# Expert rows gathered in partition quarters and turned on VectorE instead of TensorE, with empty lanes skipped

## What is computed

```
def routed_expert_mlps(x, expert_ids, gates, w_gate, w_up, w_down):
    ...
    def expert_block(args):
        tb, eb = args
        xb = x[tb]
        h = jax.nn.silu(xb @ w_gate[eb]) * (xb @ w_up[eb])
        return h @ w_down[eb]
```

## Time and profile before

| | |
|---|---|
| median of 3 runs | 2599.76 us |
| profiled execution | 2603.91 us, its span 2602.2 us |
| TensorE busy | 2333.2 us (90%) |
| VectorE, ScalarE, GpSimd busy | 1027.2, 707.5, 456.6 us |
| DMA moved | 440.35 MB, mean 169 GB/s |
| granted TensorE clock, mean over the span | 0.952 of full |

### The profile page before, as it was taken

One profiled execution on the slowest core, in us unless ns is written; L12 is line 12 of the kernel. 1 busy time (PEld: TensorE's weight loads), 2 busy tenths in 40 slices (PEclk: granted clock), 3 DMA queues, 4 the chain that ended last, 5 costly groups with the idle time before them and its releaser, 6 DMA issues. The chain is left out here.

```text
span 2602.2 us, 36339 instructions
## 1 busy us (share of the span) xinstructions
PE 2333.2 (90%) x13208; PEld 1339.2 (51%) x13208; DVE 1027.2 (39%) x1762; ACT 707.5 (27%) x1825; POOL 456.6 (18%) x632
## 2 busy tenths in 40 slices
PE   7999999999968999999999999849999999999940
PEld 3454454533546666666667666524444444444420
DVE  4415234224226554456656656341111211112128
ACT  3203122012025544345444554201111111111112
POOL 1010100100200011200131311212222212212235
PEclk9999999999978999899999999969999999999975
DMA  8041230400373112121122111167999999999967
GB/s 283 26 134 33 57 103 9 131 11 11 97 226 76 56 61 88 52 65 56 56 79 88 56 56 61 60 250 297 367 362 361 363 369 370 361 362 361 354 249 314
DMA packets 165971, 440.35 MB, mean 169 GB/s; under 512 B 36961, under 2 KB 78169, under 8 KB 141225
## 3 DMA queue, kind: packets, MB, share of 16 engines
q1 hardware_dynamic: 139351, 350.38, 37.7%
q0 software_dynamic: 20640, 70.29, 6.8%
q10 hardware_dynamic: 5842, 17.80, 1.8%
HBM read 345.11 MB, written 94.80 MB: 169 GB/s over the span
## 5 line engine op out<-in xcount | busy, mean ns | idle before, releaser
L867 PE MATMUL p_ps<-p_xt,p_w 128*128 128x512 f32 x1088 | 476.7, 597 | 0.5 <-DVE p_xt L698 0.5
L3056 PE MATMUL p_ps<-p_w_arena,p_x_arena 128*128 128x512 f32 x1024 | 446.6, 594 | 0.0
L867 PEld LDWEIGHTS p_ps<-p_xt,p_w 128*128 128x128 f32 x1088 | 205.2, 191 | 255.2 <-issue 250.0
L3056 PEld LDWEIGHTS p_ps<-p_w_arena,p_x_arena 128*128 128x128 f32 x1024 | 195.5, 191 | 245.4 <-issue 245.4
L2426 PE MATMUL p_ps<-p_w_out,p_mixt 128*128 128x512 f32 x544 | 252.5, 609 | 0.0
L3072 PE MATMUL p_ps<-p_w_arena,p_y_arena 128*128 128x512 f32 x512 | 236.0, 604 | 0.0
L2978 DVE SCALAR_TENSOR_TENSOR p_y_arena<-p_y_arena,p_ps 128x256 f32<-128x256 f32 x64 | 27.0, 422 | 459.9 <-ACT p_y_arena L2863 358.2
L2426 PEld LDWEIGHTS p_ps<-p_w_out,p_mixt 128*128 128x128 f32 x544 | 99.6, 193 | 105.8 <-issue 103.7
L876 PE MATMUL p_ps<-p_w,p_xt 128*128 128x144 f32 (+1 forms) x512 | 146.6, 440 | 0.0
L2807 POOL DMA_INDIRECT s_y<-p_y_arena,p_home x66 | 65.0, 985 | 462.3 <-PE p_ps L3043 266.6
L3072 PEld LDWEIGHTS p_ps<-p_w_arena,p_y_arena 128*128 128x128 f32 x512 | 93.1, 192 | 98.2 <-issue 93.0
(11 more groups left out here) (415 smaller groups left out, 3254.1 us busy)
## 6 DMA issues: line engine op xcount, KB each, us to landing
p_w_arena<-in_w_exp_gate SPq DMA_DIRECT2D x64, 1024.0 KB, 7.9
p_w_arena<-in_w_exp_up SPq DMA_DIRECT2D x64, 1024.0 KB, 11.1
p_w_arena<-in_w_exp_down SPq DMA_DIRECT2D x64, 1024.0 KB, 10.6
p_w_arena<-s_y SPq DMA_DIRECT2D x16, 1024.0 KB, 13.3
p_x<-in_x_prompt SPq DMA_DIRECT2D x30, 512.0 KB, 4.8
p_w<-in_w_in SPq DMA_DIRECT2D x4, 2048.0 KB, 15.5
p_spread<-s_roots SPq DMA_DIRECT2D x16, 512.0 KB, 7.1
s_kv<-p_us SPq DMA_DIRECT2D x32, 256.0 KB, 2.3
```

What stands on the lines that cost most here:

```text
L867: ins = mm(ps[:, job % 4, :], w[:, c, at:at + P], xt[s % 2][:, c, :], start=(c == 0), stop=(c == KC - 1))
L3056: t = mm(ps[:, 2 + b, :], xt[b][:, c, :], w_gu[bw][:, :, c, :], start=(c == 0), stop=(c == KC - 1))
```

## The change

- The constant `spare` marks lanes by a number past every row (`ABSENT`, 2^20). The gather and the scatter get a bounds check: a lane whose row is out of bounds is skipped. One empty lane in 32 of a gather (lane 0 of a scatter) still points to a real row.
- `hn` is written in its natural column order; the router's weights are loaded so that they fit.
- The gather of a block is four indirect DMAs, each of 128 pieces of 256 columns (1 KB). Partition 32q + b gets, in piece g, the q-th quarter of the row of lane 32g + b. `slots` therefore has four columns per block; it is built by four more matmuls that spread the list (`spread`), out of a selection matrix `sel`.
- The rows are turned by one VectorE transpose of 32 x 32 squares, whose columns are read with a step of 8 (`turn_x`). That puts feature 8p + c on partition p, as the contiguous weight transfers of 1 MB have it. The 8 TensorE transposes and their two copies are gone.
- In `moe`, TensorE's order in a pair is new, and PSUM has two banks each for `midt` and for both halves of `y`.
- The gather buffers are zeroed once (128 x 4096 by GpSimd) before the first gather.
- A listed gather reads its list five times, one column and four small squares, and has 11 small operations and two copies.

```
-                pool.indirect_dma_start(out=x[b], out_offset=None, in_=S["hn"],
-                                        in_offset=bass.IndirectOffsetOnAxis(ap=slot[b][:, 0:1], axis=0)
-                                        ).then_inc(x_in[b], 16)
+                for g in range(4):
+                    apart(pool, on["slots_ready"], 1)
+                    pool.indirect_dma_start(out=x[b][:, 256 * g:256 * g + 256], out_offset=None,
+                                            in_=S["hn"].rearrange("t (q k) -> (t q) k", q=4),
+                                            in_offset=bass.IndirectOffsetOnAxis(ap=slot[b][:, g:g + 1], axis=0),
+                                            bounds_check=4 * NTOK - 1, oob_is_err=False).then_inc(x_in[b], 16)
...
-                    pool.dma_start(raw[n][:], S["ids"][bass.ds(q, 1)].rearrange("o c -> c o")).then_inc(raw_in[n], 16)
+                    pool.dma_start(raw[n][:, 0:1], S["ids"][bass.ds(q, 1)].rearrange("o c -> c o")).then_inc(raw_in[n], 16)
+                    for k in range(4):
+                        pool.dma_start(raw[n][32 * k:32 * k + 32, 1:5],
+                                       S["ids"][bass.ds(q, 1)].rearrange("o (g b) -> b (o g)", g=4)).then_inc(raw_in[n], 16)
...
             for b in two:
                 send(b)
                 pool.wait_ge(y_out[b], 16)
+            nc.gpsimd.memset(x_arena[:, 0:R * D], 0.0).then_inc(on["x_cleared"], 1)
...
+            def turn_x(j, b, bx, x_count):
+                dve.wait_ge(x_in[bx], x_count)
+                dve.wait_ge(gu_done.sem, gu_done.back(j, 2))
+                nc.vector.transpose(xt[b].rearrange("p c (g r) -> p g c r", g=4), x[bx].rearrange("p (g a c) -> p g c a", g=4, c=KC)
+                                    ).then_inc(xt_ready.sem, 1)
...
-                stt(hn[:].rearrange("p c q -> p q c"), h[:].rearrange("p (q c) -> p q c", c=KC), hr[:],
-                    gain[:].rearrange("p (q c) -> p q c", c=KC), ALU.mult, ALU.mult).then_inc(hn_ready.sem, 1)
+                stt(hn[:].rearrange("p c q -> p (c q)"), h[:], hr[:], gain[:], ALU.mult, ALU.mult).then_inc(hn_ready.sem, 1)
...
+                        if b == 0:
+                            gate_up(j, b, bw, range(KC))
+                        else:
+                            gate_up(j, b, bw, range(KC // 2))
+                            turn_mid(j - 1, 0)
+                            gate_up(j, b, bw, range(KC // 2, KC))
...
+                    down(j, 0, bw, 0)
+                    turn_mid(j + 1, 1)
+                    down(j, 0, bw, 1)
```

More of the change, by code:

```diff
@@ L20 @@
 NT = SEQ // P
+ABSENT = 1 << 20
 DB, DT = 8, 8
@@ L2653, in moe @@
         owner = sb("owner", [1, 2 * SPILL + 1], I32)
[L2654 to L2658, removed]
+        homes = sb("homes", [P, SLOTS], I32)
+        slots = K["lg"][:].rearrange("p t n -> p (t n)")[:, 0:4 * NE].rearrange("p (g e) -> p g e", g=4)
+        sel = cut(work, 9 * D, (4, 4, 32))
+        slot = [sb(f"slot{b}", [P, 4], I32) for b in ring]
+        raw = [sb(f"raw{b}", [P, 5]) for b in two]
+        home_f, token_f, none_f = sb("home_f", [P, 1]), sb("token_f", [P, 4]), sb("none_f", [P, 4])
+        spare = sb("spare", [P, 3])
         home = [sb(f"home{b}", [P, 1], I32) for b in two]
@@ new lines, in gather_listed @@
+            def gather_listed(j, b, arrived):
+                n, ts, tt = b % 2, nc.gpsimd.tensor_scalar, nc.gpsimd.tensor_tensor
+                q = pool.value_load(owner[0:1, bass.ds(2 * (j + (R - NE)) + 1, 1)], min_val=0, max_val=NE * PLACES)
+                pool.wait_ge(xt_ready.sem, xt_ready.back(j, R))
+                apart(pool, on["slots_ready"], 1)
+                with nc.allow_non_contiguous_dma(reason="one row to columns"):
+                    pool.dma_start(raw[n][:, 0:1], S["ids"][bass.ds(q, 1)].rearrange("o c -> c o")).then_inc(raw_in[n], 16)
+                    for k in range(4):
+                        pool.dma_start(raw[n][32 * k:32 * k + 32, 1:5],
+                                       S["ids"][bass.ds(q, 1)].rearrange("o (g b) -> b (o g)", g=4)).then_inc(raw_in[n], 16)
@@ L3036, in _, with gate_up, turn_mid, down @@
             t.then_inc(on["listed"], 1)
-            def turn(j, b, bx, x_count):
-                pe.wait_ge(x_in[bx], x_count)
-                for a in range(2):
-                    pe.wait_ge(xt_act.sem if a else xt_vec.sem, xt_vec.back(j, 1))
-                    for c in range(4):
-                        t = tr(ps[:, a, c * P:(c + 1) * P], x[bx][:, (4 * a + c) * P:(4 * a + c + 1) * P], ident[:])
-                    t.then_inc(turned.sem, 1)
+            pe.wait_ge(on["sel_ready"], 1)
+            pe.wait_ge(on["token_ready"], 1)
+            for g in range(4):
+                t = mm(ps[:, 4, g * NE:(g + 1) * NE], sel[:, g].rearrange("p q b -> p (q b)"), token, start=True, stop=True)
+            t.then_inc(on["spread"], 1)
+            def gate_up(j, b, bw, chunks):
+                for c in chunks:
+                    t = mm(ps[:, 2 + b, :], xt[b][:, c, :], w_gu[bw][:, :, c, :], start=(c == 0), stop=(c == KC - 1))
+                if chunks.stop == KC:
+                    t.then_inc(gu_done.sem, 1)
+            def turn_mid(j, b):
+                pe.wait_ge(mid_ready.sem, mid_ready.all(j))
+                pe.wait_ge(midt_ready.sem, midt_ready.back(j, 2))
+                for c in range(FC):
+                    t = tr(ps[:, 7 if b else 4, c * P:(c + 1) * P], mid[b].rearrange("p (q c) -> p c q", c=FC)[:, c, :], ident[:])
+                t.then_inc(midt_turned.sem, 1)
+            def down(j, b, bw, n):
+                pe.wait_ge(y_act.sem if n else y_vec.sem, y_vec.back(j, 2))
+                for c in range(FC):
+                    t = mm(ps[:, n if b else 5 + n, :], midt[b][:, c, :], w_dn[bw][:, c, n * 512:(n + 1) * 512],
+                           start=(c == 0), stop=(c == FC - 1))
+                t.then_inc(down_done.sem, 1)
             def blocks(i):
```

178 lines of the change are left out of this document (82 added, 96 removed).

## The result

The changed kernel takes 2610.23 us (median of 13 runs, 2603.63 to 2614.96) against 2599.34 for the kernel before on the same chip (13 runs). The ratio is 1.0045, with a 95% interval from 1.0032 to 1.0058. So it is slower, by 11 us, and the interval keeps clear of no change. The forecast was 2609.

A forecast was written before the change was run, and what follows sets the result against it. TensorE was taken to bound the steady pairs, GpSimd both ends. -42.4 + 8.0 + 47.2 - 2.0 - 0.5 = +10.3 us on the median 2599.8 made 2610.1, put at 2609; own range 2598 to 2622, wider range 2582 to 2634.

The forecast's parts named there:

- The steady pairs: Middle of the expert loop: a pair of blocks falls from 23.02 to 21.39 us; 26 pairs give -42.4 us.
- The 0.2 for the second `mid`: In each pair TensorE wants the second `mid` slightly before it is ready, losing between 0 and 0.4 us, taken as 0.2.
- What had to hide: In steady pairs, VectorE's transposes (1.6 us each), GpSimd's issues (1.0 each, about 7 of 10.7 us a block) and DMA stay covered.
- the 2 that I had named as a sign: In the changed profile, a VectorE transpose under 2 us would show the forecast right.
- rival E: VectorE reads squares so slowly, over 5 us a transpose, that the second `mid` is late: 2661 us, chance 0.03.
- Rival D: A VectorE transpose beside a GpSimd issue lengthens it up to 2.6 us: 2613 us, inside the forecast's own range and its 0.50.
- The DMA side: Steady blocks need 3.69 MB in 10.7 us, 345 GB/s; the steady 363 GB/s need not be a limit.
- rival C: Skipped lanes or 1 KB pieces still load the DMA engines, so steady pairs stay at 23.0 us: 2651 us, chance 0.05.
- The start: Up to pair 2: later `slots`, more gather pieces and later list scatters make TensorE stand 15 us; +8.0 us, bounds -7 and +17.
- The listed rounds: GpSimd's last eight rounds: each 6.95 us longer, 55.6 in all, less 7 and 1.4 us; +47.2, bounds +20 and +60.
- Rival B: Five list reads queue behind one another and weights; a loaded round loses 6 us more, four make 24: 2633 us, chance 0.13.
- Elsewhere: `hn` written in order, 1.96 to about 1.25 us, 17 times, counting only where TensorE stands for it: -2.0, bounds 0 and -12.

The follow-up runs named there:

- timed alone: Only `hn` written in natural column order, router weights loaded to fit, in the kernel before: 2595.11 us, ratio 0.998, 5.1 us gained.
- mending each end alone: Two runs of the changed kernel: without any listed round 2535.53 us; with list scatters one by one between the gathers of blocks 4 to 11, 2585.89 us.
- both ends mended: No listed round and list scatters between gathers, further blocks of an expert left out: changed kernel 2515.36 us, the kernel before 2580.88 us.

## Why the prediction came out right, step by step

**The steady pairs** were forecast at 21.39 and are 21.13. The 1.83 us counted for the row transposes account for nearly all of the 1.89 gained. The 0.2 for the second `mid` was not lost: from 1850 to 2360 us TensorE's weight load waits for it 17 times, 10.6 us in all (longest 0.7), but the matmuls ahead last over that, and TensorE stays at 100 of 100 us. The term was 7 us too small.

**What had to hide** did. The transpose is 2.03 us, beyond my 1.6 and just over the 2 that I had named as a sign, but far under the 5 from which it would cost (rival E). The issue is 1.00 as priced. Rival D's lengthened issue is not there. Here is one that runs beside a transpose for 0.93 of its 1.00 us:

```profile
1740.72 2.01 DVE L2990 STREAM_TRANSPOSE p_x_arena<-p_x_arena 128x1024 f32<-128x1024 f32 x1 [0.33 <-DMA p_x_arena<-s_hn,p_slot]
...
1741.80 1.00 POOL L2766 DMA_INDIRECT p_x_arena<-s_hn,p_slot  x1 [0.30 <-issue]
```

Of the 272 issues 40 run at least in part beside a transpose, and the longest of these is 1.06 us. The longest of all, 1.20, are first issues behind list operations, like the 1.18 above, with no transpose beside them.

One inference of the prediction was wrong: that the cost of an issue is in going through the indices. No experiment was made for it, but the trace has a case. While `mix_prompt` runs, GpSimd scatters the lists of the other tiles, and those of the 64 sample tokens have 64 indices, not 128. The first of these rows is one of 64, the others have 128:

```profile
1482.91 0.91 POOL L1531 DMA_INDIRECT s_ids<-p_s_keys,p_place_i  x1 [1.37 <-DMA s_ids<-p_s_keys,p_place_i]
1485.20 0.98 POOL L1531 DMA_INDIRECT s_ids<-p_s_keys,p_place_i  x1 [1.38 <-DMA s_ids<-p_s_keys,p_place_i]
...
1490.50 0.97 POOL L1531 DMA_INDIRECT s_ids<-p_s_keys,p_place_i  x1 [1.44 <-DMA s_ids<-p_s_keys,p_place_i]
```

Half the indices save some 0.05 us, so most of the price goes by the instruction. That is seen for 4-byte elements only.

The Trainium skill (SBUF — State Buffer, "SBUF: two separate sides") tells of the shared port as a lock for a two-port mode; this f32 transpose shows no sign of such a lock.

**The DMA side.** The steady 363 GB/s were no limit: 396 were reached once no lane was skipped. The Trainium skill (DMA: Bandwidth & Descriptors, "Where 436 GB/s comes from") has the HBM side bind at about 358 GB/s a core, which it works out as a stack's 716 GB/s divided by two cores. This program runs on one core, and the run above stands 38 GB/s over that figure for 100 us, with weights, gathers and scatters mixed. By that figure a block with no lane skipped would take 11.7 us; it takes 10.6. Two readings of the prediction there were loose: the row has five slices at 431 to 432 GB/s and two at 437, not three and one; and with half the skipping (3.94 MB in 10.7 us, 368 GB/s) rival C's "2% fewer bytes" would be 1% more than 363.

**The start** was put at +8.0 and is +13.15. Relative to the last `hn` turned, `gate` and `up` of block 0 begin 2.5 us later (forecast 2), and the scatters of the lists take 33.6 us (forecast 33.7) as four long steps (5.6 to 6.4 us) and four short ones (2.4 to 2.5), as foretold. What was missing is the pause of 0.30 us before each second, third and fourth piece of a gather: 12 of them ahead of the lists make 3.6, three more in block 4's gather 0.9. These 4.5 are most of the 5.15 that the term was short of, and of the 3.7 by which the wait outgrew my 15. The pause could have been priced: the first list scatter in the earlier trace rows stands 0.31 us behind the gather's issue. The upper bound that I gave, +17, was a slip: eight steps of 6.3 us are 50.4, 16.7 more than the 33.7, and so make +25.

**The listed rounds** were put at +47.2 and are +50.0. A round without load, part by part: list reads 2.84 for 0.59 (+2.25, forecast 2.36); small operations 3.3 for 1.9 (+1.36, forecast 1.35); issues and pauses 5.1 for 1.1 (+4.06, forecast 3.24). That is 17.12 - 9.30 = 7.8 instead of 6.95, and again three pauses of 0.30 are the miss. Eight make 62.6. Against this stands the slower landing, which shrank from 31.3 to 153.87 - 8 x 17.12 = 16.9 us, 14.4 taken back where I took 7. The two errors offset each other. The scatter of block 55 came 1.8 us later after its pair's start, not 1.4 sooner: it waits 2.80 us there for the scatter before it to land. Rival B (list reads slowed by load) is thus the reverse of what happened.

**Elsewhere** is the term mis-sized most in proportion: -2.0 forecast, -5.1 timed alone, -9.25 between the two traces, of which 2.05 came before any `hn`. The principle was right: `hn` counts at few places and not 17 times. But at these places, in the two traces the fifth, the seventh and the last above all, up to 2.4 us went and not the 0.77 of one operation. Why a shorter operation gives back more than its own 0.77 us there, no run shows. The bounds, 0 and -12, held it.

So the forecast of 2609 for 2610 owes part of its closeness to luck. In the traces gains were underrated by 14 us, 2 of which aren't the change's, and costs by 10, and the two offset each other. And I took 4.1 us off because the trace of before stands above its median, while the trace of now turned out to stand on its own median. The mechanisms and their places were right. That GpSimd at both ends eats the whole gain of the pairs is shown, by mending each end alone and both together.

The Trainium skill (DMA: Bandwidth & Descriptors, "Anatomy of one DMA — SWDGE (gpsimd) path") calls descriptor generation small and variable, with the cost in the completion. In this kernel an indirect DMA of 128 indices holds GpSimd for 1.00 us, 272 times, and 0.30 pass between the pieces of a gather. How much of that is the making of descriptors the trace doesn't tell, but the issue isn't small, and the ends wait for it. The second half agrees: a list scatter's landing is waited for 1.4 to 5.5 us.

## What to carry to other kernels

Cutting one indirect transfer into four of 128 indices each costs four issues on GpSimd, whatever bytes and lanes move. Most of the price goes by the instruction: 64 indices instead of 128 take 0.91 us instead of 0.96. In the steady part it hides behind TensorE, which sets the pace, and with both ends mended the change is worth 65 us in 2581. At the ends, where other engines wait for GpSimd, it is paid in full. So before such a change look first at what GpSimd does alone at the start and the end, and take it off the path: small list transfers between the gathers instead of ahead of them, and no gathers for blocks that will not come between the last results and the tail.

## What the runs showed of the hardware

- Two indirect DMAs in a row on GpSimd have 0.30 us between them, with or without a waiting instruction there. 128 indices take 1.0 us of issue (medians 0.96 to 1.05) with 4-byte elements, 1 KB or 4 KB rows, and with or without lanes beyond the bound. With 64 indices (4-byte elements) it is 0.91.
- A transpose in 32 x 32 squares of 128 x 1024 f32, read with a step of 8, takes 2.03 us on VectorE; the arithmetic on as many columns takes 1.28 in order and 2.05 with one side permuted.
- With the DMA engines at a share of 1.01 and 396 GB/s (no lane skipped) the pairs take the same 21.13 us as at 0.88 and 341.
- Behind the wait of 18.73 us the 12 instructions of down take 7.49 us instead of 5.32, at a mean granted clock of 0.68, so partly at the lower of the two levels (1.2 and 2.4 GHz).
